# The q/k/v and gating-v projections of a two-layer diffusion backbone in 512-column tiles with half-K weight panels, and head norms over eight heads

## Chip, cores and metric

The kernel runs on one NeuronCore of one Trainium2 chip. The metric is the device time in microseconds (us) of one execution. All weights and activations are float32. Matrix products are done with a split of each float32 operand into a rounded high part and a low part (`_hi`, `_lo`, both fp32r), and three matmuls for each product (hi·hi, hi·lo, lo·hi).

## The reference, cut to what matters

128 context tokens and 256 latent tokens (384 in all, three tiles of 128) pass two layers. Each layer is a half-step SwiGLU, token mixing, and a half-step SwiGLU. The mixing of layer 0 is attention, that of layer 1 a gated MLP:

```
x  = rms_norm(h) * (1 + scale) + shift            # scale, shift, gate: silu(cond) @ mod_w + mod_b
# layer 0
qa, ka, va, qb, kb, vb = split(x @ attn_w_in)     # 512, 512, 512, 512, 128, 128 columns, K = 1024
qa, ka, qb, kb = rms_norm per head of 64, times a gain vector of 64
# neighbourhood attention (8 heads) beside grouped-query attention (8 q, 2 kv heads, rotary), then @ attn_w_out
# layer 1
u, v = split(gelu(x @ sgu_w_in))                  # 2048 and 2048 columns
v  = rms_norm(v) * v_g
sv = einsum('gts,bcsgd->bctgd', w_s, v) + b_s     # position mixing, one 128x128 matrix per group
out = (u * sv) @ sgu_w_out
```

The modulation vectors (nine of 1024 for each layer, for two conditions) come from `mod_w`, which is streamed through the whole kernel.

## The kernel before

Five instruction streams are written out by hand and meet at semaphores; the order in each stream is the program order.

**Panels.** All weights come in panels of 1 MB (128 partitions x 2048 values), numbered from 0 to 168 through the kernel. SyncE issues the transfer of panel q into `raw[q % 2]` once the low part of panel q-2 is made (`panel`, line 341). ScalarE rounds the panel to `w_hi` once TensorE is done with panel q-2 (`split`, line 520), VectorE subtracts to get `w_lo` (`split`, line 726), and TensorE waits on `lo_done`. A panel of the projections is 256 output columns over the whole K of 1024, as (k, n) with 8 x 256 values to a partition (`col_src`, line 283).

**q/k/v stage.** Nine panels in the order q, q, k, k, (gqa k and v), gqa-q, gqa-q, v, v (`QKV_ORDER`, line 1399). `token_major` (line 1072) keeps 128 tokens of x as the stationary operand and moves 256 weight columns: 3 token tiles x 8 k x 3 = 72 matmuls for a panel. The results of one panel stay in three PSUM banks, `QBANK[g % 2]`, so two panels can be in flight. `project_first` (line 1091) runs the first two panels together for the first three k, because x becomes ready k by k. From the third panel on TensorE waits until VectorE has read the banks of the panel before the last (`qkv_dve`, line 1233).

**Head norm of a panel.** ScalarE squares the panel from PSUM into `tmp` (line 614). VectorE sums the squares by head (`hms`, line 906) and scales the sums (line 910), then does the low part of the next panel (line 912). GpSimd raises the 12 sums of four heads x three tiles to the power -0.5 (`hrs`, line 503). VectorE multiplies from PSUM to SBUF (line 916), GpSimd multiplies by the gain (line 506). After four of the steps (`MOD_STEPS`, line 1401) VectorE does one modulation sum: 16 instructions over a block of `mod_w` (`mod_sum`, line 734). After the eighth step come the rotary rotation (line 887) and `mod_out`, which writes `modT` (line 925). TensorE's transposes of the heads follow the projection (line 1262); before the fifth it makes the first scores and the last modulation column sums and waits for that `modT` (lines 1267 to 1275).

**Gating-v stage.** Eight panels in the same way (line 1343), two in `project_first`. ScalarE applies Gelu from PSUM (line 681), splits the panel after the next, and squares with a running sum (line 688). VectorE splits, with a modulation sum behind each of the first four (line 977). Behind the last panel come the token norm, its power on GpSimd (line 512) and the scaled mixing matrices `wsn` (line 988), for which the first mixing matmul (line 1363) waits; one panel of the u projection lies between.

Of the kernel before, what the change touches and what calls it, by code (L numbers as in the profile page):

```python
# [29 lines left out]
P = 128  # L30
# [11 lines left out]
HD = 64  # L42
# [46 lines left out]
def build(nc, t_in, t_out, toep_dram):  # L89
# [5 lines left out]
    with ctx:  # L95
# [27 lines left out]
        mhalf = sb("mhalf", [P, 16])  # L123
        hms = sb("hms", [P, 12])
        hrs = sb("hrs", [P, 12])
# [3 lines left out]
        vss = sb("vss", [P, TT, KD])  # L129
# [43 lines left out]
        with ExitStack() as s:  # L173
            v_tok = sb("v_tok", [P, TT, SW], scope=s)
            ws_row = sb("ws_row", [P, NG, P], scope=s)
            wsT = sb("wsT", [P, NG, P], scope=s)
            wsn = sb("wsn", [P, TT, NG, P], scope=s)
            bsb = sb("bsb", [P, NG, P], scope=s)
            vsq = sb("vsq", [P, TT, 256], scope=s)
# [105 lines left out]

        FFN = [(w_gu1, w_dn1, 0), (w_gu2, w_dn2, 0), (w_gu1, w_dn1, 1), (w_gu2, w_dn2, 1)]
# [27 lines left out]
        def hsq_view(w):  # L314

            return tmp[:, 0:2, :].rearrange("p a t -> p (a t)")[:, 0:TT * w].rearrange("p (a w) -> p a w", a=TT)
# [4 lines left out]
        def heads_of(step):  # L321

            c = QKV_ORDER[step]
            if c < 2:
                return q_na[:, :, 4 * c:4 * c + 4, :], 4, 0
            if c < 4:
                return k_na[:, :, 4 * c - 8:4 * c - 4, :], 4, 1
            if c < 8:

                return qk_g[:, :, c - 6:c + 1:2, :], 4, 2  # L330
            return qk_g[:, :, NH:NH + 2, :], 2, 3
# [8 lines left out]
        def _(sp):  # L340
# [6 lines left out]
            KN = ("p (k n) -> p k n", dict(k=KD))  # L347
            JCN = ("p (j c n) -> p j c n", dict(j=1, c=2))
# [79 lines left out]
            for g in range(9):  # L428
                panel(Q_IN0 + g, 0, col_src(w_attn[0], QKV_ORDER[g]), KN)
# [5 lines left out]
            sp.wait_ge(gained, 7)  # L435
            sp.wait_ge(qkv_act, 3)
# [8 lines left out]
            for g in range(8):  # L445
                panel(Q_V + g, 0, col_src(w_sgu[0], 8 + g), KN)
# [22 lines left out]
        def _(pool):  # L469
# [29 lines left out]
            for g in range(QK_STEPS):  # L499
# [17 lines left out]
        def _(act):  # L517
# [80 lines left out]
            for g, c in enumerate(QKV_ORDER):  # L598
# [3 lines left out]
                act.wait_ge(pe_done, Q_IN0 + g + 1)  # L602
                if c in (4, 5, 8):
                    for t in range(TT):
                        dst, cols = (v_na[:, t, 256 * (c - 4):256 * (c - 4) + 256], slice(0, 256)) if c < 8 \
                            else (vg_[:, t, :], slice(128, 256))
                        last = nc.scalar.activation(dst, ps[:, QBANK[g % 2][t], cols], ACT.Copy)
                    last.then_inc(qkv_act, 1)
                if g < QK_STEPS:
                    w = heads_of(g)[1] * HD  # L610
                    if g:
                        act.wait_ge(hms_sum, g)
                    for t in range(TT):
                        last = nc.scalar.activation(hsq_view(w)[:, t, :], ps[:, QBANK[g % 2][t], 0:w], ACT.Square)
# [63 lines left out]
            for g in range(8):  # L678
                act.wait_ge(pe_done, Q_V + g + 1)
                for t in range(TT):  # L680
                    last = nc.scalar.activation(v_tok[:, t, 256 * g:256 * g + 256], ps[:, QBANK[g % 2][t], 0:256], ACT.Gelu)
                last.then_inc(gelu_v, 1)
                split(Q_V + g + 2, 0)
# [3 lines left out]
                for t in range(TT):  # L687
                    last = nc.scalar.activation(vsq[:, t, :], v_tok[:, t, 256 * g:256 * g + 256], ACT.Square,
# [30 lines left out]
        def _(dve):  # L719
# [182 lines left out]
            for g in range(8):  # L902
                if g < QK_STEPS:
                    dst, nh, _ = heads_of(g)
                    dve.wait_ge(hsq_done, g + 1)
# [3 lines left out]
                    dve.wait_ge(hms_sum, g + 1)  # L909
# [3 lines left out]
                if g < QK_STEPS:  # L913
                    dve.wait_ge(hrs_done, g + 1)
                    for t in range(TT):
                        last = nc.vector.tensor_tensor(  # L916
                            dst[:, t], ps[:, QBANK[g % 2][t], 0:nh * HD].rearrange("p (h d) -> p h d", d=HD),
                            hrs[:, t * nh:(t + 1) * nh, None].to_broadcast([P, nh, HD]), ALU.mult)
# [3 lines left out]
            dve.wait_ge(gained, QK_STEPS)  # L922
# [59 lines left out]
            dve.wait_ge(vss_done, 8)  # L982
# [34 lines left out]
        def _(pe):  # L1017
# [54 lines left out]
            def token_major(q0, banks, order, parts="hi lo"):  # L1072

                hi, lo = slot(q0)
                for t, k in order:
                    tok, cols = slice(P * t, P * t + P), slice(256 * k, 256 * k + 256)
                    out = ps[:, banks[t], 0:256]
                    if "hi" in parts:
                        mm(out, x_hi[:, k, tok], hi[:, cols], start=(k == 0), stop=False)  # L1079
                        mm(out, x_hi[:, k, tok], lo[:, cols], start=False, stop=False)  # L1080
                    if "lo" in parts:
                        last = mm(out, x_lo[:, k, tok], hi[:, cols], start=False, stop=(k == KD - 1))  # L1082
                return last if "lo" in parts else None

            def project(make, q0, i, bank):

                pe.wait_ge(lo_done, q0 + 2 * i + 1)
                tiles = 2 if make is feature_major else TT
                make(q0, bank, [(a, k) for a in range(tiles) for k in range(KD)]).then_inc(pe_done, 1)

            def project_first(make, q, banks, n):
# [362 lines left out]
```

## Time and profile before

| | us |
|---|---|
| runs, median (lowest, highest) | 1721.3 (1716.44, 1721.55) |
| profiled execution, span | 1717.1 |
| its own time, beside the span | not listed apart from the runs; the median is 4.2 above the span |
| TensorE busy | 1660.1 (97%) |
| TensorE weight load busy | 1589.1 (93%) |
| VectorE busy | 1067.5 (62%) |
| ScalarE busy | 578.3 (34%) |
| GpSimd busy | 81.3 (5%) |
| granted TensorE clock, mean | 0.976 |
| q/k/v stage, first matmul to the restart of the transposes | 359.46 to 457.36 |
| gating-v stage, first matmul to the first mixing matmul | 1202.78 to 1285.52 |

The span is from the first to the last instruction. Busy TensorE includes the overlap of pipelined matmuls, so 97% is not 97% of peak; the distance between the starts of consecutive matmuls is their real price. A granted clock of 1.00 is 2.4 GHz and 0.50 is 1.2 GHz. In a timeline row the first number is the start in us from the span's start, the second the busy time, and the bracket says how long the engine stood idle before it and which instruction released it.

### The profile page before, as it was taken

How to read it: one execution, taken by the hardware profiler on the slowest of the kernel's cores; microseconds unless marked ns; L12 is line 12 of the kernel's file. 1: busy time of each engine (PE TensorE's matmuls, PEld its weight loads, DVE VectorE, ACT ScalarE, POOL GpSimd, SP SyncE). 2: the span in 40 equal slices, each digit the busy share in tenths (PEclk: the TensorE clock that was granted, in tenths of full speed). 3: DMA queues.
4: the chain of work that ended last, by engine and by line, in shares of the span. 5: the costliest groups of instructions: out<-in, count | busy, mean ns of one | idle time of the engine just before them, and what ended most of it. 6: DMA issues, size and time to landing. Idle time of an engine off the chain costs nothing.

```text
span 1717.1 us, 25878 instructions
## 1 busy us (share of the span) xinstructions
PE 1660.1 (97%) x9927; PEld 1589.1 (93%) x9927; DVE 1067.5 (62%) x1803; ACT 578.3 (34%) x751; POOL 81.3 (5%) x48
## 2 busy tenths in 40 slices
PE   8899999988899899999989999998999998999998
PEld 4899999988756899999989999998999998999998
DVE  3677668767754766767966777697745435334323
ACT  2423232253344442322234333222642325333222
POOL 1200000034100100000010000001000001000000
PEclk9999999989999899999989999999999998999999
DMA  9755547526200445555634545564533332433332
GB/s 310 187 182 164 192 159 244 170 85 207 77 1 31 157 146 173 177 189 196 224 120 135 193 161 195 190 226 157 186 124 96 125 123 85 136 122 122 124 130 77
DMA packets 222917, 261.81 MB, mean 152 GB/s; under 512 B 14502, under 2 KB 207494, under 8 KB 222854
## 3 DMA queue, kind: packets, MB, share of 16 engines
q1 hardware_dynamic: 222854, 260.95, 46.3%
q8 instruction: 42, 0.69, 0.2%
q14 instruction: 21, 0.17, 0.0%
HBM read 258.64 MB, written 2.29 MB: 152 GB/s over the span
## 4 chain that ended last, share of the span: by engine, by line
PE 86%; issue 6%; DVE 4%; ACT 1%; POOL 1%; DMA 0%; POOLq 0%; SPq 0%; ACTq 0%; DVEq 0%
PE ps L1066 15%; PE ps L1067 15%; PE ps L1069 15%; PE ps L1022 9%; PE ps L1024 9%; PE ps L1023 9%; PE ps L1055 3%; PE ps L1037 2%; PE ps L1257 1%; DVE macc L754 1%; PE ps L1126 1%; PE ps L1294 1%; POOL hrs L503 1%; PE ps L1363 1%; DVE w_lo L731 1%
## 5 line engine op out<-in xcount | busy, mean ns | idle before, releaser
L731 DVE TENSOR_TENSOR w_lo<-raw,w_hi 128x2048 fp32r<-128x2048 f32 x164 | 380.0, 2317 | 282.3 <-ACT w_hi L527 282.2
L1066 PE MATMUL ps<-x_hi,w_hi 128*128 128x384 f32 x1536 | 523.3, 341 | 13.2 <-ACT x_hi L553 9.9
L1067 PE MATMUL ps<-x_hi,w_lo 128*128 128x384 f32 x1536 | 520.1, 339 | 0.0
L1069 PE MATMUL ps<-x_lo,w_hi 128*128 128x384 f32 x1536 | 517.1, 338 | 0.0
L527 ACT ACTIVATE w_hi<-raw 128x2048 fp32r<-128x2048 f32 x169 | 322.9, 1911 | 344.2 <-PE ps L1024 326.3
L754 DVE SCALAR_TENSOR_TENSOR macc<-mraw,cT,macc 128x256 f32<-128x256 f32 x896 | 359.9, 478 | 0.0
L1066 PEld LDWEIGHTS ps<-x_hi,w_hi 128*128 128x128 f32 x1536 | 292.1, 190 | 17.0 <-issue 13.3
L1067 PEld LDWEIGHTS ps<-x_hi,w_lo 128*128 128x128 f32 x1536 | 292.1, 190 | 0.0
L1069 PEld LDWEIGHTS ps<-x_lo,w_hi 128*128 128x128 f32 x1536 | 291.3, 190 | 0.0
L1022 PE MATMUL ps<-act_hi,w_hi 128*128 (+1 forms) x832 | 281.8, 339 | 0.0
L1024 PE MATMUL ps<-act_hi,w_lo 128*128 (+1 forms) x832 | 279.6, 336 | 0.0
L1023 PE MATMUL ps<-act_lo,w_hi 128*128 (+1 forms) x832 | 279.5, 336 | 0.0
L1022 PEld LDWEIGHTS ps<-act_hi,w_hi 128*128 128x128 f32 x832 | 156.5, 188 | 0.0
L1023 PEld LDWEIGHTS ps<-act_lo,w_hi 128*128 128x128 f32 x832 | 156.5, 188 | 0.0
L1024 PEld LDWEIGHTS ps<-act_hi,w_lo 128*128 128x128 f32 x832 | 156.4, 188 | 0.0
L569 ACT ACTIVATE act_hi<-tmp 128x768 f32 (+1 forms) x44 | 37.2, 846 | 291.4 <-DVE tmp L830 291.4
L1079 PE MATMUL ps<-w_hi,x_hi 128*128 128x256 f32 x408 | 118.0, 289 | 10.7 <-DVE qk_g L916 4.9
L830 DVE TENSOR_TENSOR tmp<-ps,tmp 128x768 f32<-128x768 f32 x44 | 42.1, 957 | 128.8 <-PE ps L1069 128.8
L1080 PE MATMUL ps<-w_lo,x_hi 128*128 128x256 f32 x408 | 116.7, 286 | 0.0
L1082 PE MATMUL ps<-w_hi,x_lo 128*128 128x256 f32 x408 | 114.6, 286 | 0.0
L565 ACT ACTIVATE tmp<-ps 128x768 f32<-128x768 f32 x44 | 35.7, 812 | 205.5 <-PE ps L1069 205.4
L1079 PEld LDWEIGHTS ps<-w_hi,x_hi 128*128 128x128 f32 x408 | 80.3, 197 | 13.3 <-issue 7.0
(154 smaller groups left out, 1310.7 us busy)
## 6 DMA issues: line engine op xcount, KB each, us to landing
raw<-ffn_w_gu SPq DMA_DIRECT2D x88, 1024.0 KB, 5.1
mraw<-mod_w SPq DMA_DIRECT2D x66, 1024.0 KB, 7.4
raw<-ffn_w_down SPq DMA_DIRECT2D x44, 1024.0 KB, 4.8
raw<-sgu_w_in SPq DMA_DIRECT2D x16, 1024.0 KB, 5.5
raw<-attn_w_in SPq DMA_DIRECT2D x9, 1024.0 KB, 5.0
raw<-sgu_w_out SPq DMA_DIRECT2D x8, 1024.0 KB, 4.8
mfirst<-mod_w SPq DMA_DIRECT2D x6, 1024.0 KB, 12.8
raw<-attn_w_out SPq DMA_DIRECT2D x4, 1024.0 KB, 4.9
```

The source lines that it names most:

```text
L527: nc.scalar.activation(w_hi[q0 % 2][:, :], raw[q0 % 2][:, :], ACT.Copy).then_inc(hi_done, 1)
L731: nc.vector.tensor_tensor(w_lo[q0 % 2][:, :], raw[q0 % 2][:, :], w_hi[q0 % 2][:, :].bitcast(F32), ALU.subtract).then_inc(lo_done, 1)
L754: last = nc.vector.scalar_tensor_tensor(acc, w, cc, acc, ALU.mult, ALU.add)
L1022: mm(out, w[0][:, cols], xs[0], start=start, stop=False)
L1023: mm(out, w[0][:, cols], xs[1], start=False, stop=False)
L1024: return mm(out, w[1][:, cols], xs[0], start=False, stop=stop)
L1066: mm(out, hi[:, cols], x_hi[:, k, :], start=(k == 0), stop=False)
L1067: mm(out, lo[:, cols], x_hi[:, k, :], start=False, stop=False)
L1069: last = mm(out, hi[:, cols], x_lo[:, k, :], start=False, stop=(k == KD - 1))
L1079: mm(out, x_hi[:, k, tok], hi[:, cols], start=(k == 0), stop=False)
L1080: mm(out, x_hi[:, k, tok], lo[:, cols], start=False, stop=False)
L1082: last = mm(out, x_lo[:, k, tok], hi[:, cols], start=False, stop=(k == KD - 1))
```

## The change

Eight of the nine q/k/v panels and all eight gating-v panels become panels of 512 output columns over half of K (4 x 512 values to a partition). Two consecutive panels make one 512-column group and accumulate in the same three PSUM banks; `GROUP_ENDS` gives the step behind which a group is complete. The fifth q/k/v panel stays as it was. Head norms go by group: eight heads (24 sums, 1536 columns) at once for q, k and gqa-q, two heads for gqa-k. ScalarE, VectorE and GpSimd do their evacuation steps behind the second half alone; the splits of every panel and the modulation sums stay at their steps. `hsq_view` takes the whole of `tmp`. The first group runs its eight k in order, in place of the shared first three (`wide_first`).

```diff
+        def wide_src(w, c0, half):
+
+            return w.rearrange("(k p) n -> p k n", p=P)[:, 4 * half:4 * half + 4, c0:c0 + 512]
...
+        def heads_of(group):
+
+            if group == 0:
+                return q_na[:, :, :, :], 8, 0
+            if group == 1:
+                return k_na[:, :, :, :], 8, 1
+            if group == 2:
+                return qk_g[:, :, NH:NH + 2, :], 2, 3
+            return qk_g[:, :, 0:NH, :], 8, 2
+
+        def by_pair(v, group):
+
+            return v.rearrange("p (s two) d -> p two s d", two=2) if group == 3 else v
...
-                panel(Q_V + g, 0, col_src(w_sgu[0], 8 + g), KN)
+                panel(Q_V + g, 0, wide_src(w_sgu[0], SW + 512 * (g // 2), g % 2), HN)
...
-            for g, c in enumerate(QKV_ORDER):
+            for g in range(9):
+                group = GROUP_ENDS.get(g)
...
-                act.wait_ge(pe_done, Q_IN0 + g + 1)
-                if c in (4, 5, 8):
+                if group is not None:
+                    act.wait_ge(pe_done, Q_IN0 + g + 1)
+                    banks = QBANK[group % 2]
...
+                if group is not None and group < QK_GROUPS:
+                    w = heads_of(group)[1] * HD
+                    if group:
+                        act.wait_ge(hms_sum, group)
                     for t in range(TT):
-                        last = nc.scalar.activation(hsq_view(w)[:, t, :], ps[:, QBANK[g % 2][t], 0:w], ACT.Square)
+                        last = nc.scalar.activation(hsq_view(w)[:, t, :], ps[:, banks[t], 0:w], ACT.Square)
                     last.then_inc(hsq_done, 1)
                 if g < 8:
                     split(Q_IN0 + g + 2, 0)
...
-            for g in range(8):
-                act.wait_ge(pe_done, Q_V + g + 1)
+            for g in range(4):
+                split(Q_V + 2 * g + 2, 0)
+                act.wait_ge(pe_done, Q_V + 2 * g + 2)
                 for t in range(TT):
-                    last = nc.scalar.activation(v_tok[:, t, 256 * g:256 * g + 256], ps[:, QBANK[g % 2][t], 0:256], ACT.Gelu)
+                    last = nc.scalar.activation(v_tok[:, t, 512 * g:512 * g + 512], ps[:, QBANK[g % 2][t], :], ACT.Gelu)
                 last.then_inc(gelu_v, 1)
-                split(Q_V + g + 2, 0)
+                split(Q_V + 2 * g + 3, 0)
                 act.wait_ge(gelu_v, g + 1)
                 if g:
                     act.wait_ge(vss_done, g)
                 for t in range(TT):
-                    last = nc.scalar.activation(vsq[:, t, :], v_tok[:, t, 256 * g:256 * g + 256], ACT.Square,
+                    last = nc.scalar.activation(vsq[:, t, :], v_tok[:, t, 512 * g:512 * g + 512], ACT.Square,
...
             for g in range(8):
-                if g < QK_STEPS:
-                    dst, nh, _ = heads_of(g)
+                group = GROUP_ENDS.get(g)
+                if group is not None:
+                    dst, nh, _ = heads_of(group)
+                    dve.wait_ge(hsq_done, group + 1)
...
                 split(Q_IN0 + g + 2, 0)
-                if g < QK_STEPS:
-                    dve.wait_ge(hrs_done, g + 1)
+                if group is not None:
+                    dve.wait_ge(hrs_done, group + 1)
                     for t in range(TT):
+                        src = ps[:, QBANK[group % 2][t], 0:nh * HD]
+                        scale = hrs[:, t * nh:(t + 1) * nh, None].to_broadcast([P, nh, HD])
...
+                        last = nc.vector.tensor_tensor(by_pair(dst[:, t], group), src, scale, ALU.mult)
                     last.then_inc(qkv_dve, 1)
                 if g in MOD_STEPS:
                     mod_sum(MOD_M + MOD_STEPS.index(g), 0)
-            dve.wait_ge(gained, QK_STEPS)
+            dve.wait_ge(gained, QK_GROUPS)
...
+            def token_major(q0, banks, w, k0, ks, tiles=range(TT), parts="hi lo"):
 
                 hi, lo = slot(q0)
+                for t in tiles:
+                    for k in ks:
+                        tok, cols = slice(P * t, P * t + P), slice(w * (k - k0), w * (k - k0) + w)
+                        out = ps[:, banks[t], 0:w]
+                        if "hi" in parts:
+                            mm(out, x_hi[:, k, tok], hi[:, cols], start=(k == 0), stop=False)
+                            mm(out, x_hi[:, k, tok], lo[:, cols], start=False, stop=False)
+                        if "lo" in parts:
+                            last = mm(out, x_lo[:, k, tok], hi[:, cols], start=False, stop=(k == KD - 1))
                 return last if "lo" in parts else None
...
+            def wide_first(q, banks, n):
+
+
+                for half in range(2):
+                    pe.wait_ge(lo_done, q + half + 1)
+                    for k in range(4 * half, 4 * half + 4):
+                        if k == 0:
+                            pe.wait_ge(xh_done, KD * n + 1)
+                            token_major(q, banks, 512, 0, [0], parts="hi")
+                        pe.wait_ge(x_done, KD * n + k + 1)
+                        last = token_major(q + half, banks, 512, 4 * half, [k], parts="hi lo" if k else "lo")
+                    last.then_inc(pe_done, 1)
+
+            def wide(q, banks, half):
+
+                pe.wait_ge(lo_done, q + 1)
+                token_major(q, banks, 512, 4 * half, range(4 * half, 4 * half + 4)).then_inc(pe_done, 1)
...
-            project_first(token_major, Q_IN0, QBANK, 1)
+            wide_first(Q_IN0, QBANK[0], 1)
             for g in range(2, 9):
-                pe.wait_ge(qkv_dve, g - 1)
-                if g == 6:
-                    pe.wait_ge(qkv_act, 1)
-                project(token_major, Q_IN0 + g, 0, QBANK[g % 2])
+                if g == 4:
+                    pe.wait_ge(qkv_dve, 1)
+                    pe.wait_ge(lo_done, Q_IN0 + 5)
+                    token_major(Q_IN0 + 4, QBANK[0], 256, 0, range(KD)).then_inc(pe_done, 1)
+                else:
+                    group, half = {2: (1, 0), 3: (1, 1), 5: (3, 0), 6: (3, 1), 7: (4, 0), 8: (4, 1)}[g]
+                    if g == 5:
+                        pe.wait_ge(qkv_dve, 2)
+                    elif g == 7:
+                        pe.wait_ge(qkv_dve, 3)
+                        pe.wait_ge(qkv_act, 1)
+                    wide(Q_IN0 + g, QBANK[group % 2], half)
                 for b in range(MOD_IN - 1):
                     if MOD_PSUM[b] == g:
                         mod_psum(MOD_M + b, 0, 4, 4 * b, True)
-            pe.wait_ge(gained, 4)
+            pe.wait_ge(gained, 2)
...
-            project_first(token_major, Q_V, QBANK, 4)
+            wide_first(Q_V, QBANK[0], 4)
...
             for g in range(2, 8):
-                pe.wait_ge(gelu_v, g - 1)
-                project(token_major, Q_V + g, 0, QBANK[g % 2])
+                if g in (4, 6):
+                    pe.wait_ge(gelu_v, g // 2 - 1)
+                wide(Q_V + g, QBANK[g // 2 % 2], g % 2)
...
-            pe.wait_ge(gelu_v, 7)
-            project(feature_major, Q_U, 0, 0)
-            pe.wait_ge(gelu_v, 8)
+            pe.wait_ge(gelu_v, 3)
+            project(Q_U, 0, 0)
+            pe.wait_ge(gelu_v, 4)
...
-QKV_ORDER = (0, 1, 2, 3, 8, 6, 7, 4, 5)
-QK_STEPS = 7
+QKV_PANEL = ((0, 0), (0, 1), (512, 0), (512, 1), (2048, None), (1536, 0), (1536, 1), (1024, 0), (1024, 1))
+GROUP_ENDS = {1: 0, 3: 1, 4: 2, 6: 3, 8: 4}
+QK_GROUPS = 4
 MOD_STEPS = (3, 4, 6, 7)
 MOD_PSUM = (5, 6, 8, 8)
```

## Rows read from the trace of the kernel before

**Rows 1.** The page's chain of work that ended last, shares of the span.
```profile
PE 86%; issue 6%; DVE 4%; ACT 1%; POOL 1%; DMA 0%; POOLq 0%; SPq 0%; ACTq 0%; DVEq 0%
```

**Rows 2.** Timeline, TensorE, q/k/v stage: start us, busy us, instruction, [idle before <-releaser].
```profile
371.10 0.28 PE L1079 MATMUL ps<-w_hi,x_hi 128*128 128x256 f32 x1
...
374.50 0.28 PE L1079 MATMUL ps<-w_hi,x_hi 128*128 128x256 f32 x1
...
379.46 0.38 PE L1079 MATMUL ps<-w_hi,x_hi 128*128 128x256 f32 x1 [1.05 <-DVE q_na L916]
...
457.36 0.90 PE L1281 MATMUL ps<-ident,q_na 128*128 128x128 f32 x3 [3.90 <-DVE modT L762]
```

**Rows 3.** Timeline, VectorE, q/k/v stage (same columns).
```profile
402.69 2.20 DVE L751 TENSOR_SCALAR macc<-mraw,cT 128x256 f32<-128x256 f32 x2
...
410.35 0.54 DVE L906 TENSOR_REDUCE hms<-tmp 128x6 f32<-128x384 f32 x1
...
414.51 0.69 DVE L916 TENSOR_TENSOR qk_g<-ps,hrs 128x128 f32<-128x128 f32 x3 [1.22 <-POOL hrs L503]
...
415.11 1.37 DVE L751 TENSOR_SCALAR macc<-mraw,cT 128x256 f32<-128x256 f32 x2
...
421.94 0.94 DVE L906 TENSOR_REDUCE hms<-tmp 128x12 f32<-128x768 f32 x1
...
423.00 2.28 DVE L731 TENSOR_TENSOR w_lo<-raw,w_hi 128x2048 fp32r<-128x2048 f32 x1
...
427.44 1.08 DVE L916 TENSOR_TENSOR qk_g<-ps,hrs 128x256 f32<-128x256 f32 x3 [2.16 <-POOL hrs L503]
...
445.67 0.60 DVE L751 TENSOR_SCALAR macc<-mraw,cT 128x256 f32<-128x256 f32 x2
...
451.74 0.88 DVE L896 TENSOR_TENSOR tmp<-qk_g,ropeT 128x320 f32<-128x320 f32 x2
```

**Rows 4.** Timeline, ScalarE, q/k/v stage.
```profile
396.72 0.94 ACT L614 ACTIVATE tmp<-ps 128x256 f32<-128x256 f32 x3 [5.75 <-PE ps L1082]
...
448.78 0.60 ACT L623 ACTIVATE kT_na<-ps 128x512 f32<-128x512 f32 x1
...
449.27 0.48 ACT L623 ACTIVATE qT_na<-ps 128x384 f32<-128x384 f32 x1
```

**Rows 5.** Timeline, TensorE, end of the gating-v stage.
```profile
1259.73 0.36 PE L1079 MATMUL ps<-w_hi,x_hi 128*128 128x256 f32 x1
...
1276.78 0.34 PE L1066 MATMUL ps<-x_hi,w_hi 128*128 128x384 f32 x1
...
1285.52 0.57 PE L1363 MATMUL ps<-wsn,v_tok 128*128 128x128 f32 x3 [0.25 <-DVE wsn L988]
```

**Rows 6.** Timeline, TensorE, two starts, 15 matmuls apart, in a gate panel.
```profile
141.08 0.34 PE L1066 MATMUL ps<-x_hi,w_hi 128*128 128x384 f32 x1
...
143.68 0.34 PE L1066 MATMUL ps<-x_hi,w_hi 128*128 128x384 f32 x1
```

**Rows 7.** Timeline, TensorE, two-pass fp32 matmuls of the attention.
```profile
505.08 0.59 PE L1310 MATMUL ps<-pT_lat,v_na 128*64 128x256 f32 x2
...
505.51 0.59 PE L1311 MATMUL ps<-pT_lat,v_na 128*64 128x256 f32 x2
```

**Rows 8.** Timeline, GpSimd, q/k/v stage.
```profile
398.93 2.27 POOL L503 TENSOR_TENSOR hrs<-hms,mhalf 128x12 f32<-128x12 f32 x1 [2.72 <-DVE hms L910]
...
402.86 1.88 POOL L506 TENSOR_TENSOR k_na<-k_na,gain 128x768 f32<-128x768 f32 x1 [1.66 <-DVE k_na L916]
...
411.18 3.30 POOL L503 TENSOR_TENSOR hrs<-hms,mhalf 128x6 f32<-128x6 f32 x1 [6.44 <-DVE hms L910]
...
415.27 1.06 POOL L506 TENSOR_TENSOR qk_g<-qk_g,gain 128x384 f32<-128x384 f32 x1 [0.80 <-DVE qk_g L916]
...
423.17 4.24 POOL L503 TENSOR_TENSOR hrs<-hms,mhalf 128x12 f32<-128x12 f32 x1 [6.84 <-DVE hms L910]
```

**Rows 9.** Windows: us, busy and count by engine (PE, PEld, DVE, ACT, POOL), PEclk, DMA, GB/s.
```profile
428.60:432.80 4.20, 4.20 (x20) 4.20 (x21) 4.02 (x3) 0.00 (x0) 4.09 (x2) 0.50 0.24 97
```

More of the change, by code:

```diff
@@ L122, in build @@
         rs = sb("rs", [P, TT])
-        mhalf = sb("mhalf", [P, 16])
-        hms = sb("hms", [P, 12])
-        hrs = sb("hrs", [P, 12])
+        mhalf = sb("mhalf", [P, 24])
+        hms = sb("hms", [P, 24])
+        hrs = sb("hrs", [P, 24])
         nmax = sb("nmax", [P, 4])
@@ L428, in _ @@
             for g in range(9):
-                panel(Q_IN0 + g, 0, col_src(w_attn[0], QKV_ORDER[g]), KN)
+                c0, half = QKV_PANEL[g]
+                if half is None:
+                    panel(Q_IN0 + g, 0, col_src(w_attn[0], c0 // 256), KN)
+                else:
+                    panel(Q_IN0 + g, 0, wide_src(w_attn[0], c0, half), HN)
                 for b in range(MOD_IN):
@@ L498, in _ @@
             pool.wait_ge(gain_done, 2)
-            for g in range(QK_STEPS):
+            for g in range(QK_GROUPS):
                 dst, nh, gn = heads_of(g)
@@ L908, in _ @@
                                             AX.X, ALU.add).then_inc(hms_sum, 1)
-                    dve.wait_ge(hms_sum, g + 1)
+                    dve.wait_ge(hms_sum, group + 1)
                     nc.vector.tensor_scalar(hms[:, 0:TT * nh], hms[:, 0:TT * nh], 1.0 / HD, EPS, ALU.mult, ALU.add) \
@@ L912, in _ @@
                 split(Q_IN0 + g + 2, 0)
-                if g < QK_STEPS:
-                    dve.wait_ge(hrs_done, g + 1)
+                if group is not None:
+                    dve.wait_ge(hrs_done, group + 1)
                     for t in range(TT):
-                        last = nc.vector.tensor_tensor(
-                            dst[:, t], ps[:, QBANK[g % 2][t], 0:nh * HD].rearrange("p (h d) -> p h d", d=HD),
-                            hrs[:, t * nh:(t + 1) * nh, None].to_broadcast([P, nh, HD]), ALU.mult)
+                        src = ps[:, QBANK[group % 2][t], 0:nh * HD]
+                        scale = hrs[:, t * nh:(t + 1) * nh, None].to_broadcast([P, nh, HD])
+                        if group == 3:
+                            src = src.rearrange("p (two s d) -> p two s d", two=2, d=HD)
+                            scale = hrs[:, t * nh:(t + 1) * nh].rearrange("p (two s) -> p two s", two=2)[:, :, :, None] \
+                                .to_broadcast([P, 2, nh // 2, HD])
+                        else:
+                            src = src.rearrange("p (h d) -> p h d", d=HD)
+                        last = nc.vector.tensor_tensor(by_pair(dst[:, t], group), src, scale, ALU.mult)
                     last.then_inc(qkv_dve, 1)
@@ L1070, in feature_major @@
                 return last if "lo" in parts else None
-            def token_major(q0, banks, order, parts="hi lo"):
+            def token_major(q0, banks, w, k0, ks, tiles=range(TT), parts="hi lo"):
                 hi, lo = slot(q0)
[L1075 to L1082, printed above, removed]
-                return last if "lo" in parts else None
@@ L1087, in project @@
+            def wide(q, banks, half):
+                pe.wait_ge(lo_done, q + 1)
+                token_major(q, banks, 512, 4 * half, range(4 * half, 4 * half + 4)).then_inc(pe_done, 1)
+            def project(q0, i, bank):
                 pe.wait_ge(lo_done, q0 + 2 * i + 1)
-                tiles = 2 if make is feature_major else TT
-                make(q0, bank, [(a, k) for a in range(tiles) for k in range(KD)]).then_inc(pe_done, 1)
-            def project_first(make, q, banks, n):
-                tiles = range(2 if make is feature_major else TT)
+                feature_major(q0, bank, [(a, k) for a in range(2) for k in range(KD)]).then_inc(pe_done, 1)
@@ L1095, in project_first @@
+            def project_first(q, banks, n):
+                make = feature_major
+                tiles = range(2)
                 shared = 3
```

46 lines of the change are left out of this document (17 added, 29 removed).

## The prediction

> **What bounds the kernel now.** I read first the page's chain of work that ended last: 86% of it is TensorE [rows 1], so the end moves only where TensorE itself gets shorter or waits. The change touches two stretches, the q/k/v projection (359 to 457 us of the span) and the gating-v projection (1203 to 1286 us). Then the timelines of the first stretch, engine by engine. TensorE stands 3.9 us until VectorE has written modT and restarts at 457.36 us [rows 2]; VectorE, from the end of the fourth panel on, has head norms, lo-splits, four modulation sums (0.60 us for the first two instructions, 6.07 us in all from 445.67 to 451.74) and the rotation one after another, and the restart follows its last instruction [rows 3]. So from the fourth panel's end (ScalarE's squares at 396.72 [rows 4]) to 457.36 the q/k/v stage is a VectorE chain with GpSimd powers in it, 60.6 us long, and TensorE's 40 us of matmuls lie beside it. The gating-v stage is the reverse: TensorE never rests from 1203 to 1285 us, then goes on at 1285.52, 0.2 us after the scaled mixing matrices are ready [rows 5].
>
> **Matmul price.** The column count streamed is the same; 72 matmuls of 256 columns per panel become 36 of 512. The trace has no 512-column fp32r matmul. Matmuls of 256 columns start 113.3 ns apart in some panels (30 in 3.40 us, from 371.10 to 374.50 [rows 2]) and 118 in others (144 in 17.05 us with one restart [rows 5]); 384 columns are 173.3 apart (15 in 2.60 us [rows 6]). At 2.4 GHz 384 columns stream in 160 ns, so the overhead is 13.3 ns there against 6.6 or 11 at 256: it grows with width. For 512 I bound: two-pass fp32 matmuls that also stream 512 column-cycles start 215 to 216 ns apart (two in 0.43 us [rows 7]), the low end; the fastest straight line, 173.3 + 60, gives 233, the high end. In between lie a constant overhead (226.7) and a proportional one (231). I take 230 ns, nearest to the 384-column row, of the same type. A pair of 256 costs 226.6 or 236 today, so wide tiles gain 6 ns a pair in the slow panels and lose 3 in the fast ones: almost nothing.
>
> The Trainium skill's page "TensorE: Matmul & The Clock Gate", section "Wait — 56ns, not 53.3ns?", puts the start-to-start of warm matmuls at N / 2.4 GHz plus about 2.5 ns. Rows 7 agree; the 384-column row does not (162.5 by the rule, 173.3 in [rows 6]). By the rule 512 columns would cost 215.8 ns; that is a rival below.
>
> **Gating-v.** Six panels beyond the first two: 216 pairs x 6 ns = -1.3 us; the first two, some 61 warm pairs, +0.2. The tail behind the last panel (now from 1276.78 to 1285.52, 8.74 us, with an 8.3 us up-panel beside it [rows 5]) gets longer: ScalarE evacuates 3 x 512 columns instead of 3 x 256 before it splits the next weights. 3 x 256 take 0.94 us; one of 512 takes 0.60 and the next can start 0.49 after it [rows 4], so 3 x 512 take 0.60 + 2 x 0.49 = 1.58, +0.64. The wider squares (+0.6) end before the lo-split that follows does. With the tail 9.4 us against 8.3 of TensorE work, TensorE waits about a microsecond. Sum: -1.1 + 0.6 = -0.4 us (rounded). VectorE's lo-splits and sums there stay as they are. Half-K panels are still 1 MB, in longer rows; their transfers lie a whole panel ahead, cost nothing, and gain nothing.
>
> **q/k/v, until the k heads are projected.** The two wide q half-panels need no evacuation between them and the k panels use other banks, so the stall at 379.46 (1.05 us, 1.2 between starts [rows 2]) goes. Matmuls of four panels: -0.2 us at 230 ns. The chain's start moves from 396.72 to 395.2. The q norm itself (10 us) lies beside the k panels (16.6 us) and is free.
>
> **q/k/v, the chain.** With GpSimd between them, widths do not simply add. I price one wide group (24 head-rows, 1536 columns) from the rows:
> - squares 1.58 (as above).
> - reduce: 0.54 us for 384, 0.94 for 768 [rows 3], so 1.74 for 1536; from its start to the lo-split's start 1.06 now (421.94 to 423.00), 1.86 then.
> - GpSimd power: 3.30 us for 6 values, 4.24 for 12 [rows 8], both with the lo-split issued 0.17 us earlier: 0.157 us a value, so 6.12 for 24. Where the power starts ahead of the lo-split it took 2.27 for 12 (398.93 [rows 8]). The new k group has reduce 1.74 against ScalarE's split 1.8 us, so the lo-split is ready just before the power; I take the slow order for both wide groups.
> - scaling from PSUM: 0.69 for 3 x 128, 1.08 for 3 x 256 [rows 3], so 1.8 for 3 x 512.
> From reduce to scaled heads: 1.86 + 0.17 + 6.12 + 0.03 + 1.8 = 9.98 us.
> - gain multiply on GpSimd: 1.06 us for 384 columns, 1.88 for 768 [rows 8], so 3.45 for 1536. It is off the chain itself, but the first two instructions of the next modulation sum take 0.60 us undisturbed and 2.20 beside a 1.88 us gain (402.69 [rows 3]). So a sum behind a wide group takes 6.07 + 1.6 + 1.6 = 9.26.
>
> The chain from the k group's end: squares 1.58, group 9.98, first sum 9.26, small group 4.76 (410.35 to 415.11), second sum 6.83 (415.11 to 421.94), a lo-split alone 2.2, gqa-q group 9.98, third sum 9.26, lo-split 2.2, fourth sum 6.07, rotation to restart 5.62 (451.74 to 457.36) [rows 2, 3]: 67.7 us. From 395.2 that is 462.9 against 457.36: +5.6 us. Of this, +3.3 is that the k and gqa-q norms now come whole where the first halves lay beside TensorE or cost less, +3.2 the longer gains ahead of the sums, +0.6 the wider squares, -1.5 the earlier start.
>
> The added waits of TensorE lie beside this chain. Panel 5 (first gqa-q half) waits for the k scaling at 406.7 while panel 4 ends near 403.2: 3.5 us, and the sixth panel waits for its lo-split, queued behind the first sum, until 418.8, so that even a restart at half clock, as from 428.6 to 432.8 us now (granted 0.50 [rows 9]), has time to be made good. The queues of SP keep their order, and its blocks of modulation weights land before the sums ask.
>
> The page "SBUF — State Buffer", section "Who interferes with whom", in the Trainium skill says that VectorE and GpSimd share a port pair which the first taker keeps for its whole instruction. That speaks against wide GpSimd instructions; the trace agrees at the widths it has (2.20 against 0.60 us [rows 3]), and no row here shows 1536.
>
> **Sum.** +5.6 - 0.4 = +5.2 us on the profiled execution, whose span is 1717.1 us; everything behind is TensorE in order and keeps the shift. Its own whole time is not shown beside the span; the three runs have a median of 1721.3, 4.2 above the span. So 1721.3 + 5.2 = 1726.5 us. A change under 0.3% (5.2 us) cannot be told from none, so the forecast sits on that edge.
>
> **Rivals.**
> A. Fast wide matmuls, 216 ns apart. For: [rows 7]. Against: [rows 6], the same type. Gating-v gains 277 warm matmuls x 14 ns = 3.9 more, the chain starts 132 x 14 ns = 1.8 earlier: 5.2 - 5.7 = -0.5, 1720.8 us. Chance 0.15.
> B. The other side: GpSimd does not pay for width. If the power comes ahead of the lo-split (as at 398.93) and costs 2.27 us whatever its width, each of two wide groups is 6.12 - 2.27 = 3.85 cheaper: 5.2 - 7.7 = -2.5, 1718.8 us; with A as well, 1713. It decides at the start of the power, whether it is before or after the lo-split's. For: one such row. Against: 6 and 12 values differ by 0.94 us, and VectorE's order favours the lo-split. Chance 0.10 (a third of it with A).
> C. Clock. TensorE's new gaps (3.5 us before panel 5, near 5 before the restart) take it to 1.2 GHz, and the transposes and scores after the restart run at half rate for longer than now: +3 us, 1729.5. For: the level of 0.50 behind a present wait [rows 9]. Against: the wait before the restart is only about a microsecond longer than today's 3.9 [rows 2]. Chance 0.20.
> D. Forecast, chance 0.55.
>
> The range: from A with a small error, 1717, to C with 233 ns matmuls (+1.6) and a bit, 1732. Slower by over 0.3%: C and nearly half of D, 0.42. Faster by over 0.3%: B with A and surprises, 0.10. The rest, 0.48, is no measurable change.
>
> **What would show it.** Wide matmuls 230 ns apart (226 to 233); no gap between the second and third panel; a gap of 3 to 4 us ahead of panel 5; powers of about 6 us on 24 values and gains of 3.4; modulation sums of 9.3 us behind the k and gqa-q groups; TensorE's restart behind modT 5 to 6 us later than 457.4; the mixing matmuls of the gating unit at an unchanged distance, within 1 us, from the start of their stage. I am wrong if the powers stay near 4 us, if TensorE, not VectorE, sets the restart, or if 512-column matmuls come out below 220 ns.

## The result, and the profile after

The changed kernel takes 1742.5 us (median of four runs, 1742.0 to 1745.4) against 1720.3 (four runs, 1716.4 to 1721.6): ratio 1.0133, 95% interval [1.0117, 1.0148], slower by 1.3%. Forecast was 1726.5 in a range of 1717 to 1732, so the time lies outside it. The span went from 1717.1 to 1740.9 us, +23.8, at the same mean granted clock of 0.976.

The page after: the chain of work that ended last, still TensorE in its largest part (as [rows 1]), and the costliest matmul group (in each group busy us, mean ns of one | idle before).

```profile
PE 85%; issue 6%; DVE 4%; POOL 1%; SPq 1%; ACT 1%; DMA 1%; POOLq 0%; ACTq 0%; DVEq 0%
...
L1087 PE MATMUL ps<-x_hi,w_hi 128*128 128x384 f32 x1536 | 526.3, 343 | 12.1 <-ACT x_hi L564 9.9
```

That group is a gate and up matmul which the diff does not touch. It stood at 523.3 us before. Its busy time overlaps with its neighbours', so the starts say more. Two starts 15 matmuls apart in a gate panel, TensorE's timeline (start us, busy us, instruction):

```profile
138.88 0.34 PE L1087 MATMUL ps<-x_hi,w_hi 128*128 128x384 f32 x1
...
141.52 0.34 PE L1087 MATMUL ps<-x_hi,w_hi 128*128 128x384 f32 x1
```

That is 2.64 us for 15, or 176.0 ns each, where [rows 6] have 2.60 us, or 173.3 ns. The time from one start to the next is called the spacing below. Each trace holds some 7,100 spacings between back-to-back 384-column matmuls of the projections; their mean is 173.3 ns before and 176.0 ns after. 7,100 x 2.66 ns = 18.9 us, spread over the whole kernel.

Stage by stage, from TensorE's starts at the same places of both programs (us; ffn is a SwiGLU half-step; third row: the changed kernel with its inputs moved to another address, experiment g3 below):

```
from - to                        first up-  q/k/v -   restart -  2nd half's  gating-v   mixing -
                                 q/k/v      restart   next ffn   ffns        - mixing   output
before                           308.4      97.9      137.4      608.1       82.7       423.2
after                            315.4      103.5     138.2      614.8       82.7       430.0
after, inputs 512 B further      311.2      103.8     137.1      608.3       83.4       423.0
384-column spacings              1,540      1         224        3,100       47         2,290
```

So +5.6 us arose in the q/k/v stage, none in the gating-v stage, and the rest in stages whose instructions are unchanged. The differences between the first two lines add up to 26.9 us and not to 23.8, because the table begins at the first up-projection matmul, and that one starts 3.3 us earlier in the changed kernel (47.82 against 51.10 us). The first stage varies by itself: 308.4 to 312.1 us in the eight kernels below and above with 173.3 ns throughout. So do the two changed stages: with the instruction order and the spacing of before, q/k/v takes 96.9 to 97.9 us and gating-v 82.6 to 83.3 us.

The q/k/v stage itself, to be read against [rows 2], [rows 3], [rows 4] and [rows 8]. TensorE: the first wide matmul, the wait ahead of panel 5, a wait for a lo-split, and the restart.

```profile
363.20 0.76 PE L1101 MATMUL ps<-w_hi,x_hi 128*128 128x512 f32 x1 [2.37 <-ACT x_hi L564]
...
410.49 0.51 PE L1101 MATMUL ps<-w_hi,x_hi 128*128 128x512 f32 x1 [3.26 <-DVE k_na L939]
...
433.65 0.47 PE L1101 MATMUL ps<-w_hi,x_hi 128*128 128x512 f32 x1 [1.24 <-DVE w_lo L745]
...
466.66 0.90 PE L1329 MATMUL ps<-ident,q_na 128*128 128x128 f32 x3 [4.44 <-DVE modT L776]
```

VectorE, k group and gqa-q group: the sum of squares by head (L921), the scaling (L939), the modulation sum behind it (its first two instructions at L765, the other 14 at L768), and at the end the rotation (L910).

```profile
400.33 1.75 DVE L921 TENSOR_REDUCE hms<-tmp 128x24 f32<-128x1536 f32 x1 [4.42 <-ACT tmp L627]
...
408.55 1.88 DVE L939 TENSOR_TENSOR k_na<-ps,hrs 128x512 f32<-128x512 f32 x3 [4.06 <-POOL hrs L514]
410.35 3.82 DVE L765 TENSOR_SCALAR macc<-mraw,cT 128x256 f32<-128x256 f32 x2
414.09 5.62 DVE L768 SCALAR_TENSOR_TENSOR macc<-mraw,cT,macc 128x256 f32<-128x256 f32 x14
419.63 0.54 DVE L921 TENSOR_REDUCE hms<-tmp 128x6 f32<-128x384 f32 x1
...
433.43 1.74 DVE L921 TENSOR_REDUCE hms<-tmp 128x24 f32<-128x1536 f32 x1
...
443.43 3.87 DVE L765 TENSOR_SCALAR macc<-mraw,cT 128x256 f32<-128x256 f32 x2
...
461.04 0.88 DVE L910 TENSOR_TENSOR tmp<-qk_g,ropeT 128x320 f32<-128x320 f32 x2
```

GpSimd, one power of 24 values (L514) and the gains of 1536 columns (L517) for q and k:

```profile
393.79 5.48 POOL L517 TENSOR_TENSOR q_na<-q_na,gain 128x1536 f32<-128x1536 f32 x1 [2.00 <-DVE q_na L939]
402.37 6.14 POOL L514 TENSOR_TENSOR hrs<-hms,mhalf 128x24 f32<-128x24 f32 x1 [3.10 <-DVE hms L925]
410.51 3.51 POOL L517 TENSOR_TENSOR k_na<-k_na,gain 128x1536 f32<-128x1536 f32 x1 [2.00 <-DVE k_na L939]
```

ScalarE's squares of the k group, where the chain starts:

```profile
398.72 1.57 ACT L627 ACTIVATE tmp<-ps 128x512 f32<-128x512 f32 x3 [6.39 <-PE ps L1104]
```

In the gating-v stage (against [rows 5]) wide matmuls run back to back; between the second and the third row below lie 12 spacings in 2.79 us, 232.5 ns each:

```profile
1219.73 0.77 PE L1101 MATMUL ps<-w_hi,x_hi 128*128 128x512 f32 x1 [2.37 <-ACT x_hi L564]
...
1249.72 0.40 PE L1104 MATMUL ps<-w_hi,x_lo 128*128 128x512 f32 x1
...
1252.51 0.39 PE L1104 MATMUL ps<-w_hi,x_lo 128*128 128x512 f32 x1
...
1302.45 2.80 PE L1412 MATMUL ps<-wsn,v_tok 128*128 128x128 f32 x23 [0.75 <-DVE wsn L1009]
```

### The profile page after: what moved, and what is told of

The parts are those of the page before. It is cut to its first block, busy times and chain, and to the rows that moved or that the text cites. A ratio compares the mean times of both kernels' runs of the same rounds, so it can differ in the third digit from the quotient of the medians.

```text
span 1740.9 us, 24644 instructions
## 1 busy us (share of the span) xinstructions
PE 1677.3 (96%) x9351; PEld 1580.8 (91%) x9351; DVE 1066.7 (61%) x1788; ACT 575.0 (33%) x703; POOL 82.1 (5%) x42
## 4 chain that ended last, share of the span: by engine, by line
PE 85%; issue 6%; DVE 4%; POOL 1%; SPq 1%; ACT 1%; DMA 1%; POOLq 0%; ACTq 0%; DVEq 0%
PE ps L1087 15%; PE ps L1088 15%; PE ps L1090 15%; PE ps L1043 9%; PE ps L1044 9%; PE ps L1045 9%; PE ps L1076 3%; PE ps L1305 1%; DVE macc L768 1%; PE ps L1342 1%; PE ps L1166 1%; POOL hrs L514 1%; SPq L414 1%; DVE macc L765 1%; DMA raw<-ffn_w_gu 1%
## 5 line engine op out<-in xcount | busy, mean ns | idle before, releaser
L768 DVE SCALAR_TENSOR_TENSOR macc<-mraw,cT,macc 128x256 f32<-128x256 f32 x896 | 360.0, 478 | 0.0
L1101 PE MATMUL ps<-w_hi,x_hi 128*128 128x512 f32 (+1 forms) x216 | 85.5, 396 | 10.4 <-ACT x_hi L564 4.7
L1102 PE MATMUL ps<-w_lo,x_hi 128*128 128x512 f32 (+1 forms) x216 | 84.6, 392 | 0.0
L1104 PE MATMUL ps<-w_hi,x_lo 128*128 128x512 f32 (+1 forms) x216 | 83.7, 391 | 0.0
L1076 PEld LDWEIGHTS ps<-ones,macc 128*128 128x128 f32 x520 | 66.9, 191 | 9.1 <-DVE macc L768 8.2
```

Of the source, the lines that this page charges most:

```text
L768: last = nc.vector.scalar_tensor_tensor(acc, w, cc, acc, ALU.mult, ALU.add)
L1076: last = mm(ps[:, bank, bass.ds(col + 2 * a + cond, 1)], macc[:, b0 % 2, cond, P * a:P * a + P], ones[:, 0:1], start=alone, stop=True, ski ...
```

## The experiments

**The question.** Why does a matmul that nobody changed start 2.7 ns later? The diff also resizes small tensors that stand in SBUF between the weight slots and the projection inputs (a part of the diff, cut):

```
-        mhalf = sb("mhalf", [P, 16])
-        hms = sb("hms", [P, 12])
-        hrs = sb("hrs", [P, 12])
+        mhalf = sb("mhalf", [P, 24])
+        hms = sb("hms", [P, 24])
+        hrs = sb("hrs", [P, 24])
 ...
-        vss = sb("vss", [P, TT, KD])
+        vss = sb("vss", [P, TT, 4])
```

In the built kernels each tensor takes its size rounded up to 32 bytes, so the first three grow by 32 bytes per partition each and vss shrinks by 32: 64 bytes in sum. x_hi went from byte 111,808 to 111,872, and x_lo, act_hi, act_lo went with it; w_hi (45,184) and w_lo (61,568) stayed. The distance of x_hi from w_hi, 66,624 bytes before, leaves 64 when divided by 256, and now 128; the other pairs of inputs and weights leave the same. Theory L: the distance between a matmul's two operands in SBUF sets the spacing. Rivals: the wide tiles or their groups disturb the rest; an absolute address counts; the added room itself costs. All spacings in ns below are means over back-to-back starts in the traces; the kernel before, run beside these, had medians of 1720.2 to 1720.3 us.

### e1: the shift alone

```
 # before
         vss = sb("vss", [P, TT, KD])
+        sb("pad", [P, 16])            # 64 B per partition
```

> The kernel before with one unused tensor of 64 bytes to a partition behind vss, so that x_hi, x_lo, act_hi and act_lo begin 64 bytes later, at the addresses they have in the changed kernel; no instruction differs. Theory L (layout: the changed kernel's 18 us outside the two stages come from these addresses): 384-column matmuls 176.0 ns apart, in the pattern 175 182 176 173 174, and 1738 us. Rival C (they come from something else in the changed program): 173.3 ns and 1720 us.

1736.97 us, ratio 1.0092 [1.0075, 1.0109], with none of the change's work in it. TensorE's timeline, 15 matmuls apart, 2.64 us; mean 176.0 ns:

```profile
140.95 0.34 PE L1067 MATMUL ps<-x_hi,w_hi 128*128 128x384 f32 x1
...
143.59 0.34 PE L1067 MATMUL ps<-x_hi,w_hi 128*128 128x384 f32 x1
```

The q/k/v stage took 98.1 us, as before, although its 256-column matmuls were slower too (118.9 ns in the mean, 116.1 before): it is bound by VectorE's chain. So 16.7 of the 22.2 us are the shift; the spans of the two profiled executions differ by 18.9, and such differences scatter by a microsecond or two.

### e2: the change without the shift

```
 # after
-        hms = sb("hms", [P, 24])
-        hrs = sb("hrs", [P, 24])
+        sb("pad", [P, 32])
 ...
         act_lo = sb("act_lo", [P, KF, T], F32R)
+        hms = sb("hms", [P, 24])
+        hrs = sb("hrs", [P, 24])
```

> The changed kernel with hms and hrs put behind act_lo and 128 unused bytes in their place, so that x_hi, x_lo, act_hi and act_lo lie exactly where they lay before. Theory L: 384-column matmuls 173.3 ns apart, both stages as the prediction had them, 1725 us (1720 + 5.6 for q/k/v, about 0 for gating-v). Rival C: 1742 us.

1727.37 us, ratio 1.0039 [1.0025, 1.0053]. Mean spacing 173.3 ns, 15 in 2.60 us:

```profile
141.10 0.34 PE L1088 MATMUL ps<-x_hi,w_hi 128*128 128x384 f32 x1
...
143.70 0.34 PE L1088 MATMUL ps<-x_hi,w_hi 128*128 128x384 f32 x1
```

q/k/v took 103.7 us, gating-v 83.3. What is left of the change is +7.1 us, where +5 was expected: 5.8 in q/k/v, 0.6 in gating-v, and the rest in no stage that changed.

### e3 and e4: both operands moved, and another shift

```
 # e3, before: ahead of w_hi (weights and inputs both move by 64 B)
+        sb("pad", [P, 16])
 # e4, before: behind vss (inputs move by 32 B)
+        sb("pad", [P, 8])
```

> The kernel before with 64 unused bytes ahead of w_hi, so that weights and x both move by 64 bytes (modulo 128: weights 64, x 0; before: weights 0, x 64; changed kernel: 0, 0). Theory L with a relative rule (slow where weights and x have the same place modulo 128): 173.3 ns, 1720 us. Theory L with an absolute rule (slow where x is at a multiple of 128): 176.0 ns, 1738 us. Rival C: 1720 us.

1718.29 us, ratio 0.999 [0.998, 1.0], 173.3 ns: two starts 15 apart, 2.60 us.

```profile
150.04 0.34 PE L1067 MATMUL ps<-x_hi,w_hi 128*128 128x384 f32 x1
...
152.64 0.34 PE L1067 MATMUL ps<-x_hi,w_hi 128*128 128x384 f32 x1
```

The inputs stand at the same byte as in e1 and the matmuls are fast. So neither an absolute address of the inputs nor the room as such costs; what e1 changed and e3 did not is the distance.

> The kernel before with 32 unused bytes behind vss (x at 96 modulo 128, weights at 0). Theory L with banks of 64 bytes: between, 173.3 to 176 ns, 1720 to 1738 us, and no faster than before. If address phases matter more finely, another spacing than these two, in either direction. Rival C: 1720 us.

1743.64 us, ratio 1.0134 [1.0117, 1.0151], 176.6 ns. It is the worst of all placements tried, at half the shift of e1, and above the 1720 to 1738 that were expected: the price does not lie between those of 64 and of 128.

### f4, g1, g2: how the placement repeats

Without e4, "slow where the two operands have the same place within 128 bytes" would have done for a rule up to here. The same pad with 128, 256 and 512 bytes in the kernel before:

> The kernel before with 128 unused bytes per partition ahead of the projection inputs, so that these move by 128 bytes and the weights do not. If the place within 128 bytes is what sets the spacing of the matmuls (theory L as 64 bytes of shift of one or of both have shown it), the 384-column matmuls stand 173.3 ns apart and the time is 1720 within 3 us. Rival (any shift, or the place within 256 bytes): 176 ns and 1735 or more.

1738.25 us (one run), 175.9 ns. A period of 128 bytes is out.

> The kernel before with 256 unused bytes per partition ahead of the projection inputs. Shifts of 32, 64 and 128 bytes of these against the weights were slow, none was fast. If the placement repeats every 256 bytes, the 384-column matmuls stand 173.3 ns apart and the time is 1720 within 3 us; rival (it repeats every 512 bytes, or not at all): 176 to 177 ns, 1736 to 1743.

1722.01 us (one run), 173.3 ns:

```profile
141.12 0.34 PE L1067 MATMUL ps<-x_hi,w_hi 128*128 128x384 f32 x1
...
143.72 0.34 PE L1067 MATMUL ps<-x_hi,w_hi 128*128 128x384 f32 x1
```

> The kernel before with 512 unused bytes per partition ahead of the projection inputs. If the placement repeats every 256 or 512 bytes: 173.3 ns, 1720 within 3 us. Rival (only the very distance of the kernel before is fast, or any room in that place costs): 176 ns and 1736 or more.

1719.7 us (one run), 173.3 ns. At the two shifts tried, 256 and 512, the fast spacing returns, as it would if the placement repeats every 256 bytes. Of the distances tried, inputs minus weights modulo 256, 64 is fast and 96, 128 and 192 are slow (176.6, 176.0, 175.9 ns). Why 64, and what the distances not tried would give, stays open.

### g4: does it belong to the matmul's own operands?

```
 # before
         x_lo = sb("x_lo", [P, KD, T], F32R)
+        sb("pad", [P, 16])            # moves act_hi, act_lo, not x_hi, x_lo
```

> The kernel before with 64 unused bytes behind the projection inputs, so that only what stands behind them moves (the activations act_hi and act_lo, the attention's tensors) and the inputs keep their distance to the weights. If the spacing belongs to a matmul's own two operands: 384-column matmuls on x_hi and x_lo stay at 173.3 ns, those on the activations go to 176 ns or more, some 2,700 of the 7,200, so about +7 us, 1727. Rival (a state of the whole kernel or of the unmoved weights): both alike, 1720 or 1736.

1724.43 us (one run), some 4 us more than before, where some 7 were expected. Both spacings stand in one trace. On x_hi and x_lo 173.3 ns, 15 in 2.60 us; on act_hi and act_lo 176.0, 15 in 2.64:

```profile
141.13 0.34 PE L1067 MATMUL ps<-x_hi,w_hi 128*128 128x384 f32 x1
...
143.73 0.34 PE L1067 MATMUL ps<-x_hi,w_hi 128*128 128x384 f32 x1
...
302.49 0.34 PE L1023 MATMUL ps<-act_hi,w_hi 128*128 x1
...
305.13 0.34 PE L1023 MATMUL ps<-act_hi,w_hi 128*128 x1
```

It belongs to the operands of the matmul at hand, not to a state of the kernel.

### f5: only the low weights moved against the high ones

```
 # before
         w_hi = [sb(f"w_hi{i}", [P, PW], F32R) for i in range(2)]
+        sb("pad", [P, 16])            # w_lo moves by 64 B, w_hi does not
 ...
         vss = sb("vss", [P, TT, KD])
+        sb("pad2", [P, 16])           # the inputs move by 128 B in all
```

> The kernel before with 64 unused bytes between the high and the low weight parts and none more than 64 bytes of shift for the inputs: inputs at 64 of 128 as before, high weights at 0 as before, low weights at 64. If the load of weights that share the place of the streamed inputs is what slows the next matmul, only the third of the matmuls that use the low weights is slow: 384-column matmuls 174.2 ns apart in the mean, the time about 1726. If only the high weights count: 173.3 ns, 1720; if one slow pairing slows all: 176 ns, 1736.

1724.7 us (one run), 174.1 ns on x_hi and x_lo, 173.7 on act_hi and act_lo. The number met the expectation, but its reasoning did not survive f4: by the distances modulo 256, the inputs stand at 192 from w_hi and at 128 from w_lo here, each of which is slow when both weights have it, and yet the mean is better than with either. Nor is only one matmul in three slow: in the order hi·hi, hi·lo, lo·hi of the projections on x the mean spacings behind each are 173.8, 174.4 and 174.0 ns. On act, in the order hi·hi, lo·hi, hi·lo, they are 174.0, 170.8 and 176.2. So the spacing depends on more than one pair at a time; which neighbours count is open.

### g3: room alone as the remedy

```
 # after, nothing moved
         vss = sb("vss", [P, TT, 4])
+        sb("pad", [P, 112])           # 448 B + the change's 64 B = 512 B
```

> The changed kernel, nothing of it moved, with 448 unused bytes per partition ahead of the projection inputs, so that with its own 64 these stand 512 bytes behind their place in the kernel before. If the placement repeats within 512 bytes, room alone gives back what the shift took: 173.3 ns, time 1727 as in e2_after_x0. Rival (what e2_after_x0 gave back came from where the statistics stand, not from the inputs' place): 176 ns, 1742.

1726.84 us, ratio 1.0037 [1.0025, 1.0050], 173.3 ns. The two ways of undoing the shift agree: 15.1 (e2) and 15.7 us (g3) come back, and +7.1 and +6.7 stay. The stages of this run are the third row of the table above.

### f2 and f3: the chain of the head norms

The other +5.6 us. Theory S: in the q/k/v loop VectorE waits for GpSimd's power (4.06 us for a wide group, above; 1.21 for the small one) and only then does the modulation sum, the head of which GpSimd's gain then holds. So put the sum ahead of the wait:

```
 # e2's kernel (f2), the kernel before (f3)
                 split(Q_IN0 + g + 2, 0)
+                if g in MOD_STEPS:
+                    mod_sum(MOD_M + MOD_STEPS.index(g), 0)
                 if group is not None:
                     dve.wait_ge(hrs_done, group + 1)
 ...
-                if g in MOD_STEPS:
-                    mod_sum(MOD_M + MOD_STEPS.index(g), 0)
```

> The changed kernel with the projection inputs back at the bytes of the kernel before (as in e2_after_x0, 1727.4 us) and one step moved: in the q/k/v loop VectorE does the modulation sum of a panel ahead of its wait for the head statistics of GpSimd, so it lies beside the powers (6.1, 3.3 us) and no longer behind the gain. Theory S (the +5.6 of the q/k/v stage is the chain VectorE-GpSimd-VectorE of waits, in which the sum stands last): the stretch from the first q/k/v matmul to TensorE's restart behind the modulation falls from 103.7 to 96 to 98 us and the time to about 1720 to 1721. Rival (TensorE then waits for something else of the same length, the powers being set by GpSimd's queue and not by VectorE's order): the stretch stays within 1 us of 103.7 and the time at 1727.

1722.69 us, ratio 1.0013 [1.0002, 1.0025]: 4.7 us better than e2. The stretch takes 101.1 against 103.7, not the 96 to 98 of the expectation; the other 2 us of the gain are in no stage that the edit touches and are not explained. TensorE's restart (the first q/k/v matmul is at 362.52), then VectorE's timeline around the k group, and the last sum:

```profile
463.65 0.90 PE L1330 MATMUL ps<-ident,q_na 128*128 128x128 f32 x3 [4.43 <-DVE modT L777]
...
404.20 0.61 DVE L766 TENSOR_SCALAR macc<-mraw,cT 128x256 f32<-128x256 f32 x2
404.73 5.62 DVE L769 SCALAR_TENSOR_TENSOR macc<-mraw,cT,macc 128x256 f32<-128x256 f32 x14
410.27 1.88 DVE L942 TENSOR_TENSOR k_na<-ps,hrs 128x512 f32<-128x512 f32 x3
...
448.75 3.82 DVE L766 TENSOR_SCALAR macc<-mraw,cT 128x256 f32<-128x256 f32 x2
```

The wait is gone and the sum's head is 0.61 instead of 3.82. But the scaling now stands behind the sum, at 410.27, where the power (6.14 us from 402.17) had ended at 408.31; and the last gain holds the last sum as before, 3.82. Part of what was won went into these two.

> The kernel before with the same one step moved (the modulation sum of a panel ahead of VectorE's wait for the head statistics). Theory S: the same chain of waits stands in the kernel before; waits for the powers of 1.2 to 2.2 us and gains held by the sum of 1.6 us a panel go, the stretch from the first q/k/v matmul to the restart behind the modulation falls from 97.9 to 90 to 93 us and the time from 1720 to 1712 to 1716. Rival (there the chain ends on TensorE's own matmuls, the stretch falls by under 2 us): 1718 to 1721.

1718.55 us, ratio 0.9989 [0.9978, 1.0000]. The rival was right: the stretch took 96.9 us, 1.0 less than before. TensorE now waits 2.85 us for the later scaling, and its wait at the restart is down to 0.27 us from 3.90, because it arrives later:

```profile
441.40 0.58 PE L1079 MATMUL ps<-w_hi,x_hi 128*128 128x256 f32 x1 [2.85 <-DVE qk_g L918]
...
458.02 0.55 PE L1281 MATMUL ps<-ident,q_na 128*128 128x128 f32 x3 [0.27 <-DVE modT L762]
```

Even that microsecond is not shown to be the order's. e3, which has the order of before and only moved tensors, also takes 96.9 us (358.70 to 455.57), with the full wait for VectorE at its end, and 1718.29 us in all:

```profile
455.57 0.90 PE L1282 MATMUL ps<-ident,q_na 128*128 128x128 f32 x3 [4.24 <-DVE modT L763]
```

What f2 and f3 do show is that the wide tiling, with the same order as f3, needs 101.1 us where the narrow one needs 96.9.

## Why the prediction was wrong

**The step that failed** is "everything behind is TensorE in order and keeps the shift", and with it the silent assumption that matmuls not in the diff keep their 173.3 ns. TensorE is in order and 86% of the chain [rows 1], so its 7,100 unchanged 384-column matmuls were the largest term that could move; I took their price from [rows 6] and asked only what the diff does to instructions. It also moves addresses: four small tensors resized, 64 bytes in sum. That term was missing; e1 measures it alone as +16.7 us, and e2 and g3, which take it away, leave 1727.4 and 1726.8 us, against a forecast of 1726.5. That closeness is partly luck: the forecast started from a median of 1721.3, and the kernel before has 1720.2 to 1720.3, so in differences it is +7.1 and +6.7 against +5.2. No row of the trace of before shows two placements for the same shape, so the size could not have been read there. What could have been seen is that 256-column matmuls on the same tensors came at two prices, 113.3 and 118 ns, for which I looked for no cause. The distance modulo 256 alone does not set these: the one 256-column panel of the changed kernel takes 113.5 ns a matmul in e2 and 117.8 in g3, where that distance is the same, and which panels of the narrow kernel are fast differs between the kernel before, g1 and g2. At 128 (e1) no panel had the low price.

**q/k/v, right in sum and nearly in each term.** Predicted +5.6, measured +5.6 with the shift, +5.8 (e2) and +5.9 (g3) without. Its stage starts 3.73 us later than that of before (363.20 against 359.47). With that taken off, the squares start at 395.0 (395.2 predicted) and the restart is at 462.9 (462.9 predicted). Measured, with the prediction in parentheses: power 6.14 (6.12), reduce 1.75 (1.74), scaling 1.88 (1.8), gain 3.51 (3.45), squares 1.57 (1.58), sum behind a wide group 9.28, from 410.35 to the reduce at 419.63 (9.26), wait ahead of panel 5 3.26 (3.5). The rows themselves, carried on in a straight line, give 1.86 for the scaling and 3.52 for the gain; the prediction wrote both a little low. The stall between the second and third panels went. The gain of the q group took 5.48 instead of 3.45, held by the lo-split beside it, which cost nothing there. By the Trainium skill's page "SBUF — State Buffer", section "Who interferes with whom", the first taker keeps the shared port pair for its whole instruction; at 1536 columns the trace now agrees, with 3.82 us for the first two instructions of a sum, which take 0.60 alone.

**Gating-v, -0.4 predicted, 0.0 measured,** +0.6 to +0.7 with the placement of before, which is no more than this stage varies in kernels with the order of before. The tail's wait came about as expected (0.75 us ahead of the mixing matmuls). The matmuls gained less: 233.3 ns at the placement of before against the 230 taken, so a pair of 118 ns saves 2.7 and not 6.

**Rivals.** A (216 ns) is out: the wide matmuls took 232.4 ns in the changed kernel and 233.3 in e2 and g3. The rule in the Trainium skill's page "TensorE: Matmul & The Clock Gate", section "Wait — 56ns, not 53.3ns?", would make 215.8 of 512 columns; for this operand type the trace does not agree at any of the three widths. B is out, the powers took 6.1 us. C came half: behind the wait at 410.49 the granted clock was 0.63, while behind the restart it was 0.73, about as before (0.71). Neither cost is visible: the chain ended where it was forecast, and from the restart to the next ffn the changed kernel took 137.1 us at the placement of before (g3) and the kernel before 137.4. The windows, two of the changed kernel and the last of the kernel before (us, busy and count of PE, PEld, DVE, ACT, POOL, granted clock, DMA share, GB/s):

```profile
410.60:414.00 3.40, 3.40 (x10) 2.72 (x11) 3.40 (x2) 0.00 (x0) 3.40 (x1) 0.63 0.00 0
...
466.60:472.00 5.40, 4.97 (x30) 4.61 (x30) 3.28 (x10) 4.40 (x13) 0.00 (x0) 0.73 0.01 3
...
457.40:462.00 4.60, 4.60 (x29) 4.40 (x30) 2.86 (x9) 3.70 (x12) 0.00 (x0) 0.71 0.00 0
```

Neither the forecast nor a rival held a layout term, so the range, drawn from them, could not hold it either.

## What to carry to other kernels

When a diff resizes any tensor ahead of the big operands, list the addresses before and after: here a shift of 64 bytes between what TensorE loads and what it streams made every 384-column fp32r matmul 1.5% slower, a shift of 32 bytes 1.9%, and padding gave it back. Compare the spacing of a matmul shape that the diff does not touch first, before any explanation of the stages. A change to tiling is only measured once the operands stand where they stood: here it costs 0.4%, not 1.3%. The distances found good here are measured for this kernel alone.

Wider groups in a chain of waits between VectorE and GpSimd lengthen every link that cannot start before the group is whole, and a longer GpSimd instruction can hold VectorE's next one for its whole length (3.82 us instead of 0.60 beside a gain of 3.51).

## What the hardware showed that was not expected

- Back-to-back fp32r matmuls of 384 columns start 173.3 ns apart, or 175.9 to 176.6, by the distance of their operands in SBUF modulo 256 bytes (64 fast; 96, 128, 192 slow). The spacings repeat in exact patterns, for instance 173 173 174 ns at 64 (before) and 173 175 175 181 176 at 128 (e1).
- The effect is the other way round, and small, at 512 columns: 232.4 ns at a distance of 128, 233.3 at 64.
- 256-column matmuls come panel by panel at 113.4 or 117.8 ns at one and the same distance modulo 256 (before, g1, g2); what switches them is open.
- A GpSimd power costs 0.157 to 0.158 us more for each further value of a partition, from 6 to 24 values, with VectorE's lo-split issued just ahead of it: 3.30, 4.24, 6.14 us. Where the power came first, 12 values took 2.27 [rows 8]; no run shows 24 values that way.
